# Row gathers of the last stage begun at other blocks of the weight build

## What is computed

```python
def block(args):                       # one block of 128 tokens
    xt, et, gt = args                  # tokens, expert numbers, expert weights: 8 heads x top 16
    act = jnp.einsum('td,tkd->tk', xt, u_tab[et])
    return jnp.einsum('tk,tkd->td', jax.nn.gelu(act, approximate=False) * gt, v_tab[et])
```

## Time and profile before

| | us |
|---|---|
| median of 3 runs | 1755.38 |
| lowest, highest | 1753.05, 1757.65 |
| the profiled execution | 1757.79 |
| its span in the trace | 1756.0 |
| the build in the span | about 540 to 666 |
| the dense loop | about 666 to 1740 |

### The profile page before, as it was taken

One profiled execution on the slowest core, in us unless ns is written; L12 is line 12 of the kernel. 1 busy time (PEld: TensorE's weight loads), 2 busy tenths in 40 slices (PEclk: granted clock), 3 DMA queues, 4 the chain that ended last, 5 costly groups with the idle time before them and its releaser, 6 DMA issues.

```text
span 1756.0 us, 29836 instructions
## 1 busy us (share of the span) xinstructions
PE 1672.2 (95%) x9344; PEld 1407.8 (80%) x9344; DVE 1558.6 (89%) x3197; ACT 871.7 (50%) x2431; POOL 654.2 (37%) x642
## 2 busy tenths in 40 slices
PE   6999999999947998899999999999999999999997
PEld 4566778866636887799999999999999998999996
DVE  3887863499999997899999999999999999999998
ACT  3222574337787984444444444444444444444443
POOL 0000000034549983344444444444444444443442
PEclk9999999999977999899999999999999999999999
DMA  8343202211125799999999999999999999999996
GB/s 353 133 144 108 73 1 87 68 53 60 48 72 157 208 284 353 364 414 398 400 408 398 395 400 388 401 410 390 399 408 404 394 403 402 397 406 403 400 392 212
DMA packets 130372, 508.73 MB, mean 290 GB/s; under 512 B 8704, under 2 KB 65152, under 8 KB 81024
## 3 DMA queue, kind: packets, MB, share of 16 engines
q0 software_dynamic: 36864, 268.45, 38.1%
q1 hardware_dynamic: 93152, 239.30, 36.7%
q10 hardware_dynamic: 288, 0.13, 0.0%
HBM read 479.21 MB, written 27.92 MB: 289 GB/s over the span
## 4 chain that ended last, share of the span: by engine, by line
PE 38%; DVE 23%; DMA 19%; issue 15%; ACT 2%; POOL 1%; DVEq 1%; SPq 0%; POOLq 0%; ACTq 0%
DMA slab<-table,ixr 16%; PE psum L840 7%; PE psum L496 7%; PE psum L854 7%; DVE slab L1727 6%; PE psum L819 5%; PE psum L731 3%; DVE ulo L1618 3%; DMA g_dram<-slab 2%; DVE slab L1717 2%; PE psum L497 2%; DVE vlo L1704 2%; PE psum L661 1%; DVE slab L1712 1%; DVE slab L1532 1%
## 5 line engine op out<-in xcount | busy, mean ns | idle before, releaser
L1842 POOL DMA_INDIRECT slab<-table,ixr x256 | 423.8, 1656 | 624.2 <-DVE slab L1727 564.3
L840 PE MATMUL psum<-hhi,uhi 128*128 128x384 f32 x1008 | 341.0, 338 | 11.9 <-issue 11.7
L840 PE MATMUL psum<-hhi,ulo 128*128 128x384 f32 x1008 | 339.9, 337 | 0.0
L840 PE MATMUL psum<-hlo,uhi 128*128 128x384 f32 x1008 | 339.4, 337 | 0.0
L1727 DVE SCALAR_TENSOR_TENSOR slab<-slab,cf 128x1024 f32<-128x1024 f32 x252 | 323.1, 1282 | 14.5
L1717 DVE SCALAR_TENSOR_TENSOR slab<-slab,h2tok 128x1024 f32<-128x1024 f32 x256 | 311.9, 1218 | 22.2 <-DMA slab<-table,ixr 22.0
L854 PE MATMUL psum<-vhi,wlo 128*128 128x512 f32 x762 | 299.0, 392 | 0.0
L854 PE MATMUL psum<-vlo,whi 128*128 128x512 f32 x762 | 298.7, 392 | 0.0
L854 PE MATMUL psum<-vhi,whi 128*128 128x512 f32 x762 | 296.4, 389 | 0.4 <-issue 0.4
L496 PE MATMUL psum<-slab 128*128 128x512 f32 x464 | 240.6, 600 | 2.1 <-ACT slab L920 1.7
L840 PEld LDWEIGHTS psum<-hhi,uhi 128*128 128x128 f32 x1008 | 190.7, 189 | 20.9 <-issue 16.2
(11 more groups left out here) (236 smaller groups left out, 2804.0 us busy)
## 6 DMA issues: line engine op xcount, KB each, us to landing
slab<-ublk SPq DMA_DIRECT2D x64, 1024.0 KB, 9.1
slab<-vtab SPq DMA_DIRECT2D x63, 1024.0 KB
slab<-wblk SPq DMA_DIRECT2D x90, 512.0 KB, 4.5
g_dram<-slab SPq DMA_DIRECT2D x12, 2048.0 KB, 9.2
slab<-g_dram SPq DMA_DIRECT2D x31, 768.0 KB, 10.1
slab<-table,ixr POOLq DMA_INDIRECT x256, 8.5
x<-x_in SPq DMA_DIRECT2D x1, 2560.0 KB, 9.3
y_out<-x SPq DMA_DIRECT2D x4, 512.0 KB, 4.0
```

The costliest lines, as they stand in the source:

```text
L840: last = pe.matmul(psum[:, b, 0:ND], w[:, c, :], m[:, c, :], start=(m_ == 0), stop=(m_ == 3 * DC - 1))
L1842: pool.indirect_dma_start(out=rows[:, sl % GR, :], out_offset=None, in_=table, in_offset=bass.IndirectOffsetOnAxis(ap=ixr[:, half, half_co ...
```

## The change

The tuple of blocks at which the four gathers are issued becomes 20, 36, 52, 68 in place of 64, 72, 80, 88. `hot_a_split` returns 0 at these blocks, which moves the four blocks at which VectorE makes all of `hot_a`. The copy of row numbers into `ixr` moves from the start of the last third of the build (ahead of block 64) to block 20, behind that block's wait for `g_made`.

```diff
-FETCH_FROM, FETCH_STEP = 2 * P // 4, P // 4 // GR
+FETCH_AT = tuple(range(20, 20 + 16 * GR, 16))
@@ hot_a_split
-            if b >= FETCH_FROM and b % FETCH_STEP == 0:
+            if b in FETCH_AT:
                 return 0
             return 1 if b % 4 == 3 else 2
@@ GpSimd's build loop
                 pool.wait_ge(halves_set, k + 1)
-                if k == N_DENSE - 1:
-                    pool.wait_ge(row_numbers_set, 1)
-                    pool.tensor_copy(ixr[:, 0, :], idxf[:, 0:8]).then_inc(ix_copied, 1)
-                    pool.wait_ge(ix_copied, 1)
                 for b in range(k * P // 4, (k + 1) * P // 4):
                     if b >= 4:
                         pool.wait_ge(g_made, b - 3)
-                    if not hot_a_split(b):
-                        fetch_row((b - FETCH_FROM) // FETCH_STEP, 0, (b - FETCH_FROM) // FETCH_STEP)
+                    if b == FETCH_AT[0]:
+                        pool.wait_ge(row_numbers_set, 1)
+                        pool.tensor_copy(ixr[:, 0, :], idxf[:, 0:8]).then_inc(ix_copied, 1)
+                        pool.wait_ge(ix_copied, 1)
+                    if b in FETCH_AT:
+                        fetch_row(FETCH_AT.index(b), 0, FETCH_AT.index(b))
                         continue
```

## The result

The changed kernel is slower: median 1765.51 us of five runs (1762.97 to 1768.06) against 1755.38, ratio 1.0058 with a 95% interval of 1.0038 to 1.0078. Timed once more beside the kernel before on another occasion it was 1.0051 (1.0032 to 1.0069). So it costs about 9 to 10 us, 5.6 to 13.7 by the two intervals; the forecast was 1.3 us less, the range ended at 1760.

What follows compares the result with a forecast made beforehand. The prediction took VectorE, with ScalarE close behind, to bound the build and TensorE the loop. Group 10's write going out 1.7 us earlier, less 0.4 for its length, gave 1.3 less: about 1754.1 us, range 1750 to 1760.

Steps and rivals of the forecast that it cites:

- rival B: In the build, ScalarE's lags add up with writes of 12.6 us: about 1759, up to 1762 at 13.2; chance 0.23.
- What goes: 4.4 us: Without ScalarE's 4.49 us stall at block 80, group 10's write goes out at 653.36, not 657.76: 4.4 us to be had.
- What comes: 11.8 us a write: Writes of groups 1, 3, 5, 7, each with a gather wholly inside, were estimated at 11.8 us each.
- 0.7 us of catching up: After a gather, the write's remaining 1.6 MB or so move at 0.332 MB a us, not 0.290: 0.7 us back.
- upper bound (13.2): Write length if the gather holds the engines for its whole 4 us window with no catching up: 13.2 us.
- recurrence: ScalarE's lag grows by write length minus 10.67 or 10.27, recovers 0.5 between: 1.1, 2.1, 2.7, 3.7 at blocks 24 to 72.
- 3.5 that are absorbed: ScalarE lag in the build that VectorE does not notice, at full clock: 3.5 us; VectorE loses 0.2 at block 72.
- The rule beside it: By the skill page's 9 to 17 descriptors a packet, a 512-byte-piece write would hold a third to half of an engine.
- Rival C: Group 11's write slips through near 691.5 instead of landing at 695.7, 4.2 us less: 1749.9; chance 0.06.

Runs made afterwards that it cites:

- rows alone: Changed kernel with gathers back at blocks 64, 72, 80, 88 and only VectorE's full hot_a blocks at 20, 36, 52, 68: 1756.89 us, ratio 1.0007.
- one-collision kernel: Changed kernel with gathers at blocks 20, 40, 56, 72, only the first placed as in the changed kernel: 1752.0 us, ratio 0.9973.
- held gathers: Kernel before, with GpSimd waiting for group 11's write to land ahead of the third gather pair behind the build: 1753.64 us, ratio 0.9980.
- first experiment: Changed kernel with gathers at blocks 24, 40, 56, 72, the first blocks of groups, same spacing of 16: 1753.57 us, ratio 0.9982.
- seventh-block kernel: Changed kernel with gathers two blocks later, at 22, 38, 54, 70, same spacing of 16: ratio 0.9989.

## Why the prediction was wrong

The order of the argument held: the loop kept its pace, nobody waited for the four gathers' data, the waits came at blocks 24, 40, 56 and 72, each ended by the landing of a write with a gather beside it, the full blocks were free (rows alone, 1.0007), and so was the `ixr` copy (at block 20 in the one-collision kernel, 0.9973). The slower rival B is what happened, and more of it than B allowed. Two terms of the sum failed, the second by far the larger.

**What goes: 4.4 us.** That term is the 4.49 us stall of one execution, and it was taken for a property of the kernel. The second profile of before has no such wait, and neither has the profile of before with the held gathers (0.91 us at block 80 and 0.92 at block 88). The prediction saw that only the last bytes were caught and did not ask how often. From group 10's landings, 123.9 against 125.6, not having the stall is worth 1.7, and the best place for the gathers (121.6) another 2.3. Against the profiled execution the 4.4 was nearly there (4.0); against the mean of the two it is 3.2, as the ratio of the first experiment says. This term was about 1 us too large.

**What comes: 11.8 us a write.** Measured 13.1, 12.6, 12.6, 13.8 and, in the second profile, 12.5, 13.3, 12.3, 12.5. What was wrong under it is the time at which the gather's data comes. It was put some 2.5 us behind its issue, as at block 64; there the running write was at its end. Beside a fresh write it comes later. The DMA queues of the changed kernel in 563:567 and 568:572, with the gather issued at 562.49:

```profile
q1 hardware_dynamic: 2246, 1.15, 102.7%
...
q0 software_dynamic: 142, 1.04, 67.2%
q1 hardware_dynamic: 640, 0.33, 32.3%
```

The gather's bytes begin near 568.5, 6.0 us behind the issue, and fall on the last fifth of the write (the last 30 to 40% of the other three). So hardly anything of the 0.7 us of catching up was to be had, and the delay over 9.2 was 3.1 to 4.6 us in the eight writes, 3.6 on average, near the gather's whole 4 us window, which the prediction held for the upper bound (13.2).

The lag then grew over the four blocks. The prediction's own recurrence, with the measured lengths and its slacks, gives: block 24, 13.1 - 10.67 = 2.4; block 40, 1.9 + 12.6 - 10.27 = 4.2, 0.7 over the 3.5 that are absorbed; block 56, 3.0 + 12.6 - 10.67 = 4.9, 1.4 over; block 72, 3.0 + 13.8 - 10.27 = 6.5, 3.0 over. VectorE loses 5.1; measured 5.9. Group 10's write would go out at 653.36 + 5.1 + 2.5 = 661.0; measured 660.88, or 662.1 with the earlier start taken off. The one-collision kernel shows the absorbing part by itself. So the failed input is a write's length, too small by 1.2 us four times, with a threshold behind it.

The agreement of the recurrence is in part luck. With the lengths of the second profile it gives 1.8, 4.4, 4.6 and 5.2, a loss of VectorE of 3.7 and group 10's write at 659.6; measured are 6.8 and 663.27, or 662.6 brought to the same start. It falls short by 1 us in one trace and 3 in the other. Rival B had added 1 to 3 us for TensorE at the low clock after its idle times, the forecast none. The granted clock was 0.96, 0.86, 0.91 and 0.91 in the four stretches of 20 us from 580 on in the second profile, 0.95, 0.96, 1.00 and 0.91 in the first, and 1.00 in all four in the second profile of before. That fits, but no run tests it apart.

**The rule beside it.** In the changed kernel's 688:689, with gathers and group 11's write both waiting, the queues moved

```profile
q0 software_dynamic: 49, 0.40, 95.0%
q1 hardware_dynamic: 48, 0.02, 8.1%
```

packet for packet, 8 KB against 512 bytes, as in 675:680 with 227 to 217. The single packets of the trace at 688 fit one of the write's, 0.03 us, between every two of the gathers', 0.31 us each, which start every 0.33 us. The Trainium skill (DMA: Bandwidth & Descriptors, Queues, rings and completion order) has the engines take turns between queues a packet at a time, with about 9 to 17 descriptors in one. The trace agrees on the turns, and not on 9 to 17 of the write's pieces in one. The prediction's estimate from the page's count pointed to the slower rival, which came, but not by that count: by the trace's turns the write gets far less than a third of the engines while both have work.

**Rival C** (the last write slips through) did not happen by the change, and its size was real: group 11's write took 27.7, 28.1 in before, 30.0 and 27.2 in the changed kernel. In its last 6 us the few packets left, 20 in 4 us, go out between the gathers' (changed kernel, 695:699):

```profile
q0 software_dynamic: 225, 1.68, 99.3%
q1 hardware_dynamic: 20, 0.01, 0.8%
```

Holding the third pair of gathers behind the build back made that write 24.4 and 24.7 us, and gained 3.5 to 4 us each time by the ratios. Without the hold it took 24.9 to 30.6 in twelve traces.

**What stays open.** The means of two traces each put the changed kernel 5.5 us behind at group 10's landing, 6.2 at group 11's, and 5.7 at the end. The timings say 9 to 10, with lower ends of 5.6 and 6.7. The traces come near these lower ends and explain no more. The seventh-block kernel was nearly as late at group 10's landing (129.1) and by its ratio lost nothing, so that a late build costs the whole program its lateness is not shown for every kernel. What keeps a gather's first bytes back beside a fresh write was not tested. The loop itself, from the v copy behind the read-back to the end of the span, varied from 1046.4 to 1052.4 us between traces of kernels that do not differ in it, so two traces a side cannot carry 3 us. And why group 11's write took anything from 24.9 to 30.6 us where the gathers behind the build were issued at almost the same distances from it was not settled.

## What to carry to other kernels

A small transfer put beside a periodic one costs by its place in the period and by the slack of that period, not by its share of the DMA engines: here a DMA share of 0.79 looked like room, and the write's buffer had 0.7 to 1.1 us of slack. Lags in a ring of buffers add up over a threshold, so one collision in a trial shows nothing of four. And before a stall of one trace is booked as a gain, look at a second profile of the same kernel, above all where the stall hangs on the last few packets of a transfer.

## What the runs showed of the hardware

- A gather from GpSimd needed 2.3 to 2.7 us from issue to its first bytes beside a write at its end or none (eight of eight in the two profiles of before), and 5.5 to 6.2 us when issued within 1.3 us behind a write (eight of eight in the two of the changed kernel). Issued 2.5 to 5.3 us behind one it needed 3.2 to 5.9 us (seven in the seventh-block kernel and in the one with the gathers a block earlier), so that its first bytes came 8.4 to 8.8 us behind the write's issue. I had expected one figure.
- Queues with 8 KB and 512-byte packets moved them one for one while both had work (49 to 48 in a us), which leaves the small one 0.02 of 0.42 MB; a straggling last 10 KB took 4 us.
- The write alone moved 0.29 MB a us, and behind a gather often 0.33 to 0.35; not always, in the changed kernel's 573:577 it was 0.26 to 0.30.
